# Combining expert outputs by accumulating gathers instead of by sums on VectorE

## The reference, cut to what matters

```
eid, comb = hier_route(hn, ...)          # per row: 2 of 32 experts, and 2 weights
h = h + routed_experts(hn, eid, comb, w_e_gate, w_e_up, w_e_down)
y = rmsnorm(h, g_final)

# routed_experts, per block of 128 slots of one expert e:
h = silu(xblk @ w_e_gate[e]) * (xblk @ w_e_up[e])
yb = h @ w_e_down[e]
contrib = yb[dest] * comb.reshape(A)[order][:, None]
return segment_sum(contrib, st, num_segments=T)
```

## Time and profile before

| | us |
|---|---|
| median of 3 runs (2036.16 to 2038.36) | 2036.87 |
| the profiled execution's own time | 2039.37 |
| its span | 2037.5 |
| granted TensorE clock, mean over the span | 0.937 |
| TensorE matmuls busy | 1796.6 (88%) |
| VectorE busy | 1195.6 (59%) |
| ScalarE busy | 814.9 (40%) |
| POOL busy | 340.3 (17%) |
| HBM read and written | 350.10 MB and 75.53 MB |

### The profile page before, as it was taken

How to read it: one execution, slowest core, us unless ns; L and a number is a source line. 1 busy time by engine, 2 the same in 40 slices (tenths; PEclk the granted TensorE clock), 3 DMA queues, 4 the chain that set the end, 5 groups by cost and what they waited for, 6 DMA issues and landing times. The chain is left out here.

```text
span 2037.5 us, 35475 instructions
## 1 busy us (share of the span) xinstructions
PE 1796.6 (88%) x14826; PEld 1481.7 (73%) x14826; DVE 1195.6 (59%) x1320; ACT 814.9 (40%) x921; POOL 340.3 (17%) x307
## 2 busy tenths in 40 slices
PE   7999997888888885899999998827999999999980
PEld 7998885777777764688788885425888888888860
DVE  4543103677776665524333332067999999999956
ACT  5111212343443313402221210006777777777742
POOL 1322002244333330000000000002111111111105
PEclk9999998999999886999999998857999999999995
DMA  7755253122222208563001115348999999999967
GB/s 281 245 193 178 102 144 117 67 72 72 83 88 72 80 13 285 212 225 126 32 32 60 36 42 238 125 152 306 397 404 405 401 403 405 406 405 402 400 250 273
DMA packets 111972, 419.11 MB, mean 206 GB/s; under 512 B 25892, under 2 KB 44264, under 8 KB 82920
## 3 DMA queue, kind: packets, MB, share of 16 engines
q1 hardware_dynamic: 99592, 373.76, 49.2%
q0 software_dynamic: 7072, 25.69, 3.3%
q10 hardware_dynamic: 5184, 17.82, 2.1%
HBM read 350.10 MB, written 75.53 MB: 209 GB/s over the span
## 5 line engine op out<-in xcount | busy, mean ns | idle before, releaser
L2563 DVE TENSOR_TENSOR ex_wg_lo<-moe_raw,ex_wg_hi 128x2048 fp32r<-128x2048 f32 x128 | 287.3, 2283 | 10.7 <-ACT ex_wg_hi L2656 10.6
L2656 ACT CAST ex_wg_hi<-moe_raw 128x2048 fp32r<-128x2048 f32 x128 | 244.5, 1912 | 81.7 <-PE banks L2473 56.9
L2473 PE MATMUL banks<-ex_wg_hi,ex_x_hi 128*128 128x512 f32 x512 | 207.8, 406 | 12.7 <-issue 5.6
L2473 PE MATMUL banks<-ex_wg_hi,ex_x_lo 128*128 128x512 f32 x512 | 201.6, 394 | 0.0
L2473 PE MATMUL banks<-ex_wg_lo,ex_x_hi 128*128 128x512 f32 x512 | 201.2, 393 | 0.0
L2563 DVE TENSOR_TENSOR ex_wd_lo<-moe_raw,ex_wd_hi 128x2048 fp32r<-128x2048 f32 x64 | 146.3, 2287 | 54.2 <-ACT ex_wd_hi L2656 54.2
L2656 ACT CAST ex_wd_hi<-moe_raw 128x2048 fp32r<-128x2048 f32 x64 | 122.3, 1912 | 51.3 <-PE banks L2473 32.5
L2473 PEld LDWEIGHTS banks<-ex_wg_hi,ex_x_hi 128*128 128x128 f32 x512 | 97.3, 190 | 44.3 <-issue 23.4
L516 PE MATMUL banks<-pj_w_hi,pj_x_hi 128*128 128x448 f32 (+1 forms) x288 | 109.7, 381 | 11.6 <-DVE pj_x_lo L347 11.6
L2473 PEld LDWEIGHTS banks<-ex_wg_hi,ex_x_lo 128*128 128x128 f32 x512 | 97.2, 190 | 21.2
L2473 PEld LDWEIGHTS banks<-ex_wg_lo,ex_x_hi 128*128 128x128 f32 x512 | 97.5, 190 | 18.3
(11 more groups left out here) (402 smaller groups left out, 4112.8 us busy)
## 6 DMA issues: line engine op xcount, KB each, us to landing
moe_raw<-w_e_gate SPq DMA_DIRECT2D x64, 1024.0 KB, 7.4
moe_raw<-w_e_up SPq DMA_DIRECT2D x64, 1024.0 KB, 7.3
moe_raw<-w_e_down SPq DMA_DIRECT2D x64, 1024.0 KB, 7.3
blocks<-ex_y ACTq DMA_DIRECT2D x32, 512.0 KB, 7.7
mx_pin<-proj SPq DMA_DIRECT2D x8, 1664.0 KB, 6.8
h<-at_h SPq DMA_DIRECT2D x18, 512.0 KB, 2.7
at_slots<-cache_mem_k SPq DMA_DIRECT2D x8, 1024.0 KB, 11.7
at_slots<-cache_mem_v SPq DMA_DIRECT2D x8, 1024.0 KB, 7.2
```

The costliest lines, as they stand in the source:

```text
L2473: ins = pe.matmul(out, a, b, start=first and i == 0, stop=final and i == 2)
L2563: v.tensor_tensor(w_lo(j), raw[:, j], as_f32(w_hi(j)), ALU.subtract).then_inc(S_("w_split"), 1)
L2656: act.copy(w_hi(j), raw[:, j]).then_inc(S_("w_high"), 1)
```

## The change

Outputs are weighted by slot where they leave PSUM, and the gathers add to `h_rows` in SBUF. For this, VectorE multiplies `in_block` by the weights and splits the product into a high and a low part (held in the first piece of `wd_hi`, which is free then), and TensorE sums `at_slot` times these in 18 matmuls of 96 columns into PSUM bank 7, which the phase does not use otherwise; VectorE adds the two halves to `slot_w`, a weight for each slot and block. `at_slot` and `in_block` now live through both phases. `y1` and `y2` keep their space under other names (`unused`, `rest`).

```diff
@@ -2167,7 +2167,7 @@
 
-def phase_route(core, PS, dest, comb, slot_tok, over_info, raw):
+def phase_route(core, PS, dest, comb, slot_tok, over_info, raw, at_slot, in_block):
@@ -2186,8 +2186,7 @@
         block_f, slot_f = sb("block_f", [P, 2 * TILES]), sb("slot_f", [P, 2 * TILES])
-        in_block = sb("in_block", [P, 2 * TILES, NBLK])
-        at_slot, of_block = sb("at_slot", [P, 2 * TILES, CAP], F32R), sb("of_block", [P, 2 * TILES, NBLK], F32R)
+        of_block = sb("of_block", [P, 2 * TILES, NBLK], F32R)
@@ -2321,7 +2320,7 @@
 
-def phase_experts(core, PS, slot_tok, over_info, dest, comb, raw, split, final):
+def phase_experts(core, PS, slot_tok, over_info, dest, comb, raw, split, final, at_slot, in_block):
@@ -2336,7 +2335,7 @@
         wg_hi, wg_lo, wd_hi, wd_lo, x_hi, x_lo = split
-        h_rows, g_rows, y1, y2 = final
+        h_rows, g_rows, unused = final
@@ -2348,6 +2347,10 @@
         ident = sb("ident", [P, P])
+        PAIRS = 2 * TILES
+        of_weight = wd_hi[:, 0, 0:PAIRS * 2 * NBLK].rearrange("p (n a b) -> p n a b", a=2, b=NBLK)
+        slot_w = sb("slot_w", [P, NBLK])
+        WEIGHTS = 7
@@ -2454,10 +2457,13 @@
                     po.wait_ge(S_(f"y_stored{par}"), 16 * (NE // 2) + 16)
-                for t in range(TILES):
-                    for k, y in enumerate((y1, y2)):
-                        po.indirect_dma_start(y[0:rows[t], t], None, d["blocks"],
-                                              bass.IndirectOffsetOnAxis(ap=dest[0:rows[t], k, t:t + 1], axis=0)).then_inc(S_(f"y{t}"), 16)
+                po.wait_ge(S_("h_rows"), 16 * (TILES + 1))
+                for k in range(2):
+                    for t in range(TILES):
+                        if k:
+                            po.wait_ge(S_(f"y{t}"), 16)
+                        po.indirect_dma_start(h_rows[0:rows[t], t], None, d["blocks"], bass.IndirectOffsetOnAxis(ap=dest[0:rows[t], k, t:t + 1], axis=0),
+                                              compute_op=ALU.add).then_inc(S_(f"y{t}"), 16)
@@ -2519,7 +2525,15 @@
 
+                def slot_weights(pairs):
+                    for i in pairs:
+                        ins = pe.matmul(PS[:, WEIGHTS, 0:2 * NBLK], at_slot[:, i, :], of_weight[:, i].rearrange("p a b -> p (a b)"), start=i == 0, stop=i == PAIRS - 1)
+                    return ins
+
+                pe.wait_ge(S_("of_weight"), 1)
+                slot_weights(range(TILES))
                 turn_x(0, 0)
+                slot_weights(range(TILES, PAIRS)).then_inc(S_("weights_summed"), 1)
@@ -2594,9 +2608,16 @@
 
+                lk = Steps(v, S_("dve"))
+                lk(v.tensor_tensor(in_block[:], in_block[:], comb[:].rearrange("p k t -> p (k t)").unsqueeze(2).to_broadcast([P, PAIRS, NBLK]), ALU.mult))
+                lk(v.tensor_copy(of_weight[:, :, 0, :], in_block[:]))
+                v.tensor_tensor(of_weight[:, :, 1, :], in_block[:], as_f32(of_weight[:, :, 0, :]), ALU.subtract).then_inc(S_("of_weight"), 1)
...
                 rows_low(0, 0)
+                v.wait_ge(S_("weights_summed"), 1)
+                lk(v.tensor_copy(slot_w[:], PS[:, WEIGHTS, 0:NBLK]))
+                v.tensor_tensor(slot_w[:], slot_w[:], PS[:, WEIGHTS, NBLK:2 * NBLK], ALU.add).then_inc(S_("slot_w"), 1)
@@ -2618,14 +2639,6 @@
 
-                lk = Steps(v, S_("dve"))
-
-                def add(t):
-                    r = slice(0, rows[t])
-                    v.wait_ge(S_(f"y{t}"), 32)
-                    lk(v.scalar_tensor_tensor(h_rows[r, t], y1[r, t], comb[r, 0, t:t + 1], h_rows[r, t], ALU.mult, ALU.add))
-                    v.scalar_tensor_tensor(h_rows[r, t], y2[r, t], comb[r, 1, t:t + 1], h_rows[r, t], ALU.mult, ALU.add).then_inc(S_("added"), 1)
-
@@ -2637,12 +2650,9 @@
                 for t in range(TILES):
-                    add(t)
-                    if t >= 1:
-                        mean_square(t - 1)
+                    mean_square(t)
...
                         scaled(t - BEHIND)
-                mean_square(TILES - 1)
@@ -2670,7 +2680,7 @@
                     act.wait_ge(S_(f"y_stored{par}"), stored)
-                    act.copy(y[:, par], rows_out()).then_inc(S_("y"), 1)
+                    act.activation(y[:, par], rows_out(), ACT.Copy, scale=slot_w[:, bass.ds(n, 1)]).then_inc(S_("y"), 1)
@@ -2699,6 +2709,7 @@
                     high(j, 1)
+                act.wait_ge(S_("slot_w"), 1)
@@ -2716,15 +2727,15 @@
                     act.wait_ge(S_("ov_d"), j + 1)
-                    act.copy(y[:, 0], rows_out()).then_inc(S_("ov_y"), 1)
+                    act.activation(y[:, 0], rows_out(), ACT.Copy, scale=slot_w[:, bass.ds(j + NE, 1)]).then_inc(S_("ov_y"), 1)
...
                 for t in range(TILES):
-                    act.wait_ge(S_("added"), t + 1)
-                    act.activation(y1[:, t], h_rows[:, t], ACT.Square, accum_out=st[:, t, 0:1]).then_inc(S_("squares"), 1)
+                    act.wait_ge(S_(f"y{t}"), 32)
+                    act.activation(unused[:, t], h_rows[:, t], ACT.Square, accum_out=st[:, t, 0:1]).then_inc(S_("squares"), 1)
@@ -2750,12 +2761,15 @@
             split = [weights.enter_context(nc.sbuf_tensor("ex_" + n, s, F32R)) for n, s in shapes.items()]
-        final = sb("h_rows", [P, TILES, D], F32), sb("g_rows", [P, D], F32), sb("y1", [P, TILES, D], F32), sb("y2", [P, TILES, D], F32)
+        final = sb("h_rows", [P, TILES, D], F32), sb("g_rows", [P, D], F32), sb("unused", [P, TILES, D], F32)
+        sb("rest", [P, TILES, D], F32)
...
             raw = experts.enter_context(nc.sbuf_tensor("moe_raw", [P, len(PIECES), PW], F32))
-            phase_route(core, PS, dest, comb, slot_tok, over_info, raw)
+            pairs = lambda n, s, t: experts.enter_context(nc.sbuf_tensor("moe_" + n, s, t))
+            at_slot, in_block = pairs("at_slot", [P, 2 * TILES, CAP], F32R), pairs("in_block", [P, 2 * TILES, NBLK], F32)
+            phase_route(core, PS, dest, comb, slot_tok, over_info, raw, at_slot, in_block)
             core.end_phase()
-            phase_experts(core, PS, slot_tok, over_info, dest, comb, raw, split, final)
+            phase_experts(core, PS, slot_tok, over_info, dest, comb, raw, split, final, at_slot, in_block)
```

## The result

| | before | changed |
|---|---|---|
| median, us | 2036.51 (4 runs) | 2057.55 (4 runs, 2054.01 to 2058.86) |
| profiled execution, its span | 2039.37, 2037.5 | 2054.01, 2052.2 |

A forecast was written before the change was run, and what follows sets the result against it. TensorE and DMA were taken as full in the loop, gathers filling the DMA and then VectorE bounding the tail. Tail to 2054.3 plus 0.4, 1.6 and 0.1 gave 2056.4, +18.9; on the median, 2056 us, range 2041 to 2082.

The forecast's parts named there:

- An accumulating gather at 2.82 us: Tail: each full gather takes 1.52 us plus 1.30 us for reading the old row from SBUF; upper bound 4.12 us.
- 48 us for the queue: Tail, a sign to look for: the software queue's time rises to 48 us from 25.9.
- a second read that can't be hidden under a full DMA: Tail: adding also reads the old row from SBUF, 1.30 us a gather in series, as DMA engines are near full.
- ratio of 1.93: Tail: measured for reduce-scatter against all-gather; by it a gather takes an estimated 2.93 us, the end 1.9 us later.
- When the gathers end: Tail: 17 gathers of 2.82 us from 1992.1 end at 2040.0, 2040.7 with a store between, landing at 2042.1.
- +16.8 forecast: Tail alone: the end moves to 2054.3 on the profile's time line, against the span of 2037.5.
- Six scalings and the last store: Tail: six scalings, 7.3 us, stand behind the last tile's mean; then 3.45 us from last store to end.
- the doubling of the rival: Tail: POOL's entry doubles from 0.94 us, issue spacing 2.3 us; 2047 us if addition is free; included in forecast's 0.60.
- a wait as a sign to look for: Tail: POOL would wait for the DMA at the second nine gathers, which it never did before.
- The start: Start of the expert phase: first low part moves 0.4 us later, taken as +0.4, bounds -1.4 to +2.4.
- The loop: Expert loop: scaled evictions cost 0.10 us at 16 turns, +1.6 us, and +0.1 for the last; 0 to 3.3 possible.
- the 0.2 that the forecast had named as its limit: Expert loop: the prediction is wrong if the 18.2 us per expert change by more than 0.2.

The follow-up runs named there:

- The plain gathers: Changed kernel with each gather overwriting the residual rows instead of adding to them, order and waits kept: ratio 0.9985 to the kernel before, tail 46.6 us.
- the bf16 view: Changed kernel with the same gathered bytes seen as twice as many bf16 elements, residual left out: 2054.93 us in one execution.
- BEHIND 1: Changed kernel with a tile scaled one tile behind its mean instead of five: ratio 1.0088 to the kernel before, tail 66.6 us.
- the three shifts tried: Kernel before with powers between gathers and scaling four behind, 1.0008; also hidden-row weights and two accumulating gathers, 1.0021; all additions before scalings, 1.0015.

## Why the prediction was right, point by point

Forecast +18.9 us; measured +18.3 inside the phase and +21.0 by the medians. The mechanism came out as forecast; the terms did so less well than their sum.

**An accumulating gather at 2.82 us.** Measured 2.76 by the queue's time (forecast 48 us for the queue, 47.0 measured). The plain gathers show that the addition alone does it. The reason given, a second read that can't be hidden under a full DMA, fits all that was seen, and the bf16 view excludes the element rate; that it is a read was not isolated. By the Trainium skill's ratio of 1.93 (Collectives: The Full Stack, The bandwidth ceiling) it would have been an estimated 2.93; these traces have 2.76/1.52 = 1.81 by the queue's time and 2.49/1.32 = 1.89 by landings.

**When the gathers end.** The last landing was put at 2042.1 with the last eviction at 1985.42, 56.7 us after it; the last square begins at 2040.05, 53.5 after 1986.56. The stream was not even: some 1.3 us a gather were added in the first half, and landings of 2.49 followed. The one rate of 2.82 is too slow for the second half. It was built on 1.52 us for a plain gather, a mean with the slow start of the stream in it; late plain gathers took 1.32, and 1.32 + 1.30 = 2.62 is nearer to 2.49. That is the main part of the 3.3 us by which the tail was over-estimated (+16.8 forecast, +13.5 measured, with 1 us of spread in a tail).

**Six scalings and the last store.** 7.3 and 3.45 forecast, 7.25 and 3.49 measured (from 2048.71 to the end at 2052.2). The first scaling came after tile 5's square, as its order says. That stores can't be started sooner for nothing, which the forecast did not claim, was learned from BEHIND 1.

**POOL.** 1.54 us for an entry instead of 0.94, 1.84 apart: less than the doubling of the rival, and under the transfer's time. Right that it is hidden; it did not stall at the new waits either, as its row at 2022.38 shows only 0.30 before it, where the forecast had named a wait as a sign to look for. The first nine landings were always ahead of their waits.

**The start.** +0.4 forecast, 0 measured to the first expert matmul; and 0.8 us came back before the first eviction. There the matmuls of 512 columns go from 0.63 us (granted clock 0.50) to 0.39 (1.00) at 1386.4, 3.2 us after the first of them; before, at 1391.3, 4.4 us after the first. TensorE had been at work with the new small matmuls ahead of it. The bounds of -1.4 to +2.4 held the sum.

**The loop.** This is the mis-sized term: +1.7 forecast for the evictions (16 x 0.10, and the last), +5.5 measured. Each eviction showed, not every second one: 0.19 a pair, near 3 us in all. The chain of waits passes through ScalarE once in a pair, and I read from that that the other eviction was covered; it has no slack either. A further 0.12 a pair, some 1.8 us, was no term at all: two thirds of it come from where the tiles lie, since 12.7 KB a partition were put ahead of them. The last 0.9 us are the lower clock of the last expert's matmuls in this execution. The period changed by 0.16 us an expert, inside the 0.2 that the forecast had named as its limit.

The errors nearly cancel: 3.3 us too much in the tail and 1.2 too much at the start, 3.8 too little in the loop. A part of the closeness of 2056 to 2057.55 is luck.

## What to carry to other kernels

A gather that adds is not a free addition: here it took the DMA engines 1.8 to 1.9 times the time of a plain one. Moving a sum from VectorE to the DMA can be expected to pay only where the DMA engines are idle and VectorE is late; no run here shows such a case. Before taking work off an engine at the end of a kernel, ask how full the other resource is; here both were close to full, and none of the three shifts tried made the kernel faster. In a loop where several engines are close to their limit, count a lengthened instruction at each of its executions, and compare periods inside one execution rather than whole times.

## What the runs showed of the hardware

- A gather of 128 rows of 4 KB that adds in SBUF landed every 2.49 us, a plain one every 1.32 us. POOL took 1.54 us to issue it instead of 0.94, with the same packets and bytes in the queue.
- The accumulate costs by bytes, not by elements: 46.9 us for the queue with bf16 elements, 47.0 with fp32.
- The addresses of tiles alone changed 512-column matmuls of the down pieces from 392 and 394 to 398 ns in the median, and a pair of experts from 36.57 us to 36.65.
- Matmuls with 96 columns came 0.24 us apart on the lower clock of 0.50, those with 48 columns 0.22.
- Taking the scalar from an SBUF column instead of a constant cost VectorE 0.06 us (1.137 against 1.076). On ScalarE, an activation scaled by such a column took 0.10 us more than a plain copy (1.118 against 1.017); the column and the change of instruction were not taken apart.
